# Layer 0's latents in two halves: loads in another order, and the products over the lower 512 channels before chunks 1 and 3 of the modulation

## Chip, cores and metric

The kernel runs on one core of a Trainium2 chip. The metric is the device time of one execution in microseconds (us); what is compared are medians over runs.

## What is computed

Two layers of a hybrid backbone over 640 tokens of 1024 channels: 512 latent tokens (`x_sample`) and 128 context tokens (`x_prompt`). Only the head of layer 0 matters here:

```python
m_lat = jnp.split((jax.nn.silu(c) @ mod_w[l] + mod_b[l])[:, None, :], 6, axis=-1)
m_ctx = jnp.split(jax.nn.silu(c_ctx) @ mod_w[l] + mod_b[l], 6, axis=-1)
hs = xs * (1.0 + m_lat[1]) + m_lat[0]          # and hp from xp with m_ctx
q_a, f_f, f_b, i_a, g_a, cq, ckv_raw, kr = jnp.split(h @ w_in, AB_SPLITS, axis=-1)
q = (_rms_norm(cq_raw, q_norm_g) @ w_uq)       # 384 columns of cq
ckv = _rms_norm(ckv_raw, kv_norm_g)            # 256 columns, then 32 of kr
```

Shift and scale (`m[0]`, `m[1]`) are the first 2048 columns of `mod_w[0]`, four chunks of 512: chunks 0 and 1 are the shift of channels 0 to 511 and 512 to 1023, chunks 2 and 3 the scale of the same halves. The "latents" are the last 672 columns of `h @ w_in` (384 + 256 + 32). All is float32. What follows (attention, HGRN2, experts, layer 1) is not touched.

## The kernel before

The program for each engine is written out by hand; engines meet at semaphores. PSUM is cut into four slots of 128x1024 words. `psum_groups()` lists every group of matmuls in PE's order and hands the slots out in turn (slot 0, 1, 2, 3, 0, ...); `open_group` makes PE wait until the group that had the slot before has been released by the engine that reads it, `filled` makes a reader wait for PE, `release` and `emptied` are the other way round.

**Loads.** SP issues all large loads in the order of a list `items`, each into one of five weight slots of 2 MB; `load_item` first waits (`retire`) until PE has closed the last group that read the slot's old content. Before: the first 131 columns of the constants, `mod` chunks 0 to 3 (2 MB each, slots 0 to 3), token tiles 0 and 1 of X, the lower half of `cqa` (512 latent columns, channels 0 to 511, 1 MB), its upper half, `cqb` (the other 160 columns, 0.64 MB), token tiles 2 and 3, tile 4, the other constants (1.2 MB), `uq`, `ukv`. ACT's own queue issues eleven small loads for the vectors, the first two of which are `c` and `c_ctx`; POOL's issues six.

**PE.** It waits for all small vectors and the Silu on ACT (L1055), turns the vectors into columns (group `vec`, L2319 to L2321), and then, by `FIRST_MODS`, multiplies the columns of silu(c) by the weight chunks (`mod`, L2174, eight matmuls over 512 columns) and turns each result row, once DVE has copied it out (L1441), into columns (`modb`, L2183, four matmuls of two columns). The order is `mod` 0, `mod` 1, `modb` 0, `mod` 2, `modb` 1, `mod` 3, `modb` 2, X tile 0, `modb` 3, so that a turn has another product ahead of it.

**A token tile.** PE turns the eight 128x128 blocks of X (`xT`, L2196). ACT evacuates blocks 0 to 3 with scale and shift (L1022), DVE blocks 4 to 7 (L1473). PE multiplies by `cqa` and `cqb` over eight blocks of channels (`cq`, L2350, L2354, L2358 for tile 0 and L2295 for the others). ACT copies the 672 columns out (L1075), squares and sums them (L1077, L1078) and takes the roots (L1079, L1080); DVE takes reciprocals and scales (L1522 to L1525). PE turns the normed rows (`nT`, L2211 to L2216) one tile later and computes the values (`v`, L2340) of the tile before that. `nT` 5 is the cached context, `krP` (L2379) the rotation of the rope keys.

In the trace a float32 matmul stands as two records, so a group of 16 matmuls reads x32; a transpose is one record. In the profile X is `x_tm`, the turned and modulated X is `h_cm`, slots 0 to 2 are `weights`, slot 3 is `mix_cm`, `c_cm` holds silu(c), `mod_parts` the result rows, and `scratch` the latents and what is made of them.

## Time and profile before

| | us |
|---|---|
| median of 3 runs | 1297.8 |
| lowest, highest | 1297.08, 1301.81 |
| the profiled execution, its own time | 1300.3 |
| its span | 1298.4 |
| PE busy | 1197.1 (92%) |
| DVE, ACT, POOL busy | 598.1, 352.1, 193.5 |
| mean granted clock of PE | 0.97 |

The profile is of one execution. Its rows give a start and a duration in us from the start of the span; what stands in brackets is how long the engine was idle ahead and what released it. The part that the change touches is the first 100 us of 1298.

### The profile page before, as it was taken

Reading aid. Unit: us, or ns where it says so; the run is one execution under the profiler, and the core shown is the slowest. Engines: PE = TensorE matmul, PEld = TensorE weight load, DVE = VectorE, ACT = ScalarE, POOL = GpSimd, SP = SyncE. Lnnn points to the kernel's source line nnn. Section 1 sums busy time; section 2 is a strip of 40 time slices with the busy share of each in tenths; the row PEclk is TensorE's granted clock in tenths of the full one; section 3 lists DMA queues with packets and bytes.
Section 4 is the critical chain, followed back from the end, with each engine's and each line's share of the span. In section 5 each row is a group of like instructions: output and inputs, shape, how many; then the busy total and the mean of one; then the engine's idle time right before and its main releaser. Section 6 shows DMA issues by size and latency. Waiting matters only on the chain.

```text
span 1298.4 us, 17510 instructions
## 1 busy us (share of the span) xinstructions
PE 1197.1 (92%) x6755; PEld 682.6 (53%) x6755; DVE 598.1 (46%) x1173; ACT 352.1 (27%) x695; POOL 193.5 (15%) x189
## 2 busy tenths in 40 slices
PE   5999999999999989999999868999999999999774
PEld 2554555545546677455555435755555555555431
DVE  2213333310136666857332217079986866322218
ACT  1333444421214543212122115311023111121122
POOL 1000000010000001231332120800000333232220
PEclk9999999999999999998999898999999998999977
DMA  9504467873110205816799959021114338999873
GB/s 350 204 28 173 151 242 253 283 256 136 66 62 10 74 9 208 325 70 254 309 409 408 407 206 359 23 90 65 66 65 183 141 147 309 407 410 407 347 265 138
DMA packets 99666, 269.79 MB, mean 208 GB/s; under 512 B 12811, under 2 KB 15154, under 8 KB 98690
## 3 DMA queue, kind: packets, MB, share of 16 engines
q1 hardware_dynamic: 81904, 228.26, 46.7%
q0 software_dynamic: 17360, 40.31, 8.5%
q8 instruction: 54, 0.88, 0.3%
q14 instruction: 26, 0.21, 0.0%
q10 hardware_dynamic: 322, 0.12, 0.0%
HBM read 257.68 MB, written 31.93 MB: 223 GB/s over the span
## 4 chain that ended last, share of the span: by engine, by line
PE 76%; DMA 7%; DVE 6%; SPq 5%; ACT 3%; issue 2%; ACTq 0%; POOL 0%; POOLq 0%; DVEq 0%
PE ps L2284 17%; PE ps L2295 14%; PE ps L2796 8%; PE ps L2174 4%; PE ps L2813 3%; DMA ln_rows<-in_moe_w_up 3%; PE ps L2436 3%; PE ps L2599 3%; PE ps L2784 2%; SPq L710 2%; PE ps L2580 2%; SPq L708 2%; PE ps L2403 2%; PE ps L2226 1%; DMA scratch<-expert_rows 1%
## 5 line engine op out<-in xcount | busy, mean ns | idle before, releaser
L2284 PE MATMUL ps<-h_cm,weights 128*128 128x512 f32 (+1 forms) x832 | 226.8, 434 | 0.0
L2284 PEld LDWEIGHTS ps<-h_cm,weights 128*128 128x128 f32 x832 | 126.3, 191 | 104.0 <-issue 103.7
L2295 PE MATMUL ps<-weights,mix_cm 128*128 128x512 f32 x256 | 112.2, 595 | 0.0
L1768 DVE SCALAR_TENSOR_TENSOR scratch<-scratch,taps_cm 128x655 f32<-128x655 f32 x120 | 101.5, 897 | 2.5 <-ACT scratch L1324 1.0
L2295 PEld LDWEIGHTS ps<-weights,mix_cm 128*128 128x128 f32 x256 | 47.9, 190 | 56.5 <-issue 56.4
L2066 DVE TENSOR_TENSOR scratch<-ps,scratch 128x128 f32<-128x128 f32 x38 | 11.1, 291 | 142.3 <-ACT scratch L1372 142.3
L2295 PE MATMUL ps<-weights,h_cm 128*128 128x512 f32 (+1 forms) x208 | 71.4, 502 | 0.0
L2796 PE MATMUL ps<-weights,scratch 128*64 128x256 f32 x384 | 70.1, 395 | 0.2 <-DMA weights<-in_moe_w_up 0.2
L1441 DVE COPY mod_parts<-ps 128x512 f32<-128x512 f32 x24 | 16.6, 690 | 94.0 <-PE ps L2174 94.0
L1696 DVE SCALAR_TENSOR_TENSOR mix_cm<-mix_cm,gate_rows,ps 128x128 f32<-128x128 f32 x152 | 46.0, 345 | 25.1 <-PE ps L2544 23.0
L921 POOL DMA_INDIRECT expert_rows<-scratch,gather_scatter_rows x32 | 31.9, 998 | 158.3 <-ACT scratch L1362 98.9
L2295 PEld LDWEIGHTS ps<-weights,h_cm 128*128 128x128 f32 x208 | 36.3, 190 | 35.6 <-issue 35.6
L2796 PE MATMUL ps<-h_cm,scratch 128*64 128x256 f32 x208 | 49.2, 391 | 6.3 <-DMA ln_rows<-in_moe_w_up 4.7
L2796 PE MATMUL ps<-scratch 128*64 128x256 f32 x192 | 48.0, 407 | 5.9 <-DMA weights<-in_moe_w_up 5.9
L2058 DVE COPY scratch<-ps 128x512 f32<-128x512 f32 x38 | 26.3, 691 | 51.2 <-PE ps L2813 46.4
L1372 ACT ACTIVATE scratch<-ps 128x128 f32<-128x128 f32 x38 | 10.5, 277 | 143.4 <-PE ps L2796 143.4
L902 POOL DMA_DIRECT2D h_rows<-scratch x10 | 5.6, 558 | 279.4 <-DVE scratch L1854 279.4
L2796 PEld LDWEIGHTS ps<-weights,scratch 128*64 128x64 f32 x384 | 40.4, 142 | 7.1 <-DMA weights<-in_moe_w_up 0.4
L1573 DVE TENSOR_REDUCE softmax_max<-ps 128x1 f32<-128x640 f32 (+1 forms) x40 | 26.8, 711 | 30.3 <-PE ps L2436 30.1
L1354 ACT ACTIVATE scratch<-ps 128x512 f32<-128x512 f32 x38 | 22.7, 597 | 63.2 <-PE ps L2784 62.6
L2796 PEld LDWEIGHTS ps<-h_cm,scratch 128*64 128x64 f32 x208 | 28.2, 140 | 21.6 <-issue 8.9
L1362 ACT ACTIVATE scratch<-ps 128x512 f32<-128x512 f32 x38 | 22.7, 597 | 59.9 <-PE ps L2813 54.5
(451 smaller groups left out, 2149.0 us busy)
## 6 DMA issues: line engine op xcount, KB each, us to landing
weights<-in_mod_w SPq DMA_DIRECT2D x13, 2048.0 KB, 8.4
x_tm<-in_mod_w SPq DMA_DIRECT2D x10, 2048.0 KB, 8.6
weights<-in_moe_w_gate SPq DMA_DIRECT2D x24, 512.0 KB, 11.1
weights<-in_moe_w_up SPq DMA_DIRECT2D x24, 512.0 KB, 13.5
weights<-in_moe_w_down SPq DMA_DIRECT2D x24, 512.0 KB, 15.3
scratch<-in_moe_w_down SPq DMA_DIRECT2D x21, 512.0 KB, 13.3
weights<-in_ab_w_in SPq DMA_DIRECT2D x5, 2048.0 KB, 12.9
weights<-in_cd_w_in SPq DMA_DIRECT2D x5, 2048.0 KB, 18.5
```

What stands on the lines that cost most here:

```text
L921: nc.gpsimd.indirect_dma_start(out=YD[:, :], out_offset=bass.IndirectOffsetOnAxis(ap=rows, axis=0), in_=ZT[:, par, :], in_offset=None, bou ...
L1573: V.tensor_reduce(MXS[:, b, i:i + 1], ps("s", h, t)[:, 0:nk], AX.X, ALU.max, negate=True).then_inc(softmax_dve, 1)
L1696: ins = V.scalar_tensor_tensor(out=nxt, in0=state_before(i, n, step, hh), scalar=HE[:, u % 2, at:at + 1], in1=bank(4 + j)[:, hh * 128:hh * ...
L1768: ins = V.scalar_tensor_tensor(out=CO[:, j, 0:655], in0=UP[:, j, k:k + 655], scalar=CW[:, 4 * k + j:4 * k + j + 1], in1=CO[:, j, 0:655], o ...
L2058: V.tensor_copy(ZT[:, u % 2, 512:1024], result_bank(u, 1)).then_inc(m["yv"], 1)
L2174: ins = T.matmul(ps("mod", l, c)[32 * j:32 * j + 32, 0:512], CT[:, k, :], w[:, k, :], start=(k < 4), stop=(k >= 4))
L2284: ins = T.matmul(ps(*name)[:, a:b], w[:, k, col:col + 128], HT[:, k, a:b], start=(k == 0), stop=(k == KD - 1))
L2295: ins = T.matmul(ps(*name)[:, at:at + w.shape[2]], src[:, k, t * 128:t * 128 + 128], w[:, k, :], start=(k == 0), stop=(k == KD - 1))
L2436: ins = T.matmul(ps("s", 2 * p + i, t)[:, a:b], q[rows, tc], k[rows, ka:ka + b - a], start=(rope == 0), stop=(rope == 1))
L2599: ins = T.matmul(bank(3)[:, 0:256], HT[:, k, t * 128:t * 128 + 128], w[:, k, 256 * half:256 * half + 256], start=(k == 0), stop=(k == KD - 1))
L2796: ins = T.matmul(pair_bank(u)[SL * i:SL * i + SL, 0:256].rearrange("p (g f) -> p g f", g=2), XGT[:, u % 2, at:at + SL], w[:, k, :, :], sta ...
L2813: ins = T.matmul(result_bank(u, b)[SL * i:SL * i + SL, :], HIDT[:, u % 2, SL * i:SL * i + SL], w[:, b * 512:b * 512 + 512], start=True, st ...
```

## The change

It does five things.

1. SP's order becomes: constants, chunk 0 (slot 0), chunk 2 (slot 2), X tiles 0 and 1, the lower half of `cqa` (slot 1, free so far), then, once PE has done the product with chunk 2, the lower half of `cqb` (slot 2), X tiles 2 and 3, chunk 1 (slot 3), chunk 3 (slot 0), the upper halves of `cqa` and `cqb`, X tile 4, constants, `uq`, `ukv`.
2. `c` and `c_ctx` get a semaphore of their own (`d_c`). The Silu waits for these alone, and PE turns them in a group of their own (`c`) ahead of the other vectors.
3. The latents of a tile are made in two halves. `xa` t (blocks 0 to 3 of X) is evacuated by ACT, `ca` t multiplies it by the lower halves of the weights into a PSUM slot and ACT copies the 672 columns out. Later `xT` t (blocks 4 to 7) is evacuated by DVE, `cq` t multiplies by the upper halves, and DVE adds the first half while it copies out.
4. PE's order up to `ca` 4 is the list `FRONT`.
5. Semaphores: `xT` groups are released by DVE, so `h_half` is gone from the loop; `d_cache` is merged into `d_vec`.

```diff
-FIRST_MODS = [("mod", 0), ("mod", 1), ("modb", 0), ("mod", 2), ("modb", 1), ("mod", 3), ("modb", 2), ("modb", 3)]
+FRONT = [("c",), ("mod", 0, 0), ("vec",), ("modb", 0, 0), ("mod", 0, 2), ("modb", 0, 2), ("xa", 0), ("xa", 1), ("ca", 0), ("xa", 2), ("ca", 1),
+         ("xa", 3), ("ca", 2), ("mod", 0, 1), ("modb", 0, 1), ("ca", 3), ("mod", 0, 3), ("modb", 0, 3), ("xa", 4), ("xT", 0, 0), ("ca", 4)]
...
-        for c in range(4):
-            mod_item(0, c, c)
+        for c, at in ((0, 0), (2, 2), (1, 3), (3, 0)):
+            mod_item(0, c, at)
...
-                    if items[n] == ("cqa",):
-                        retire(WITEM[items[n]]["before"])
+                    if items[n] == ("mod", 0, 1):
+                        sp.dma_start(X[:, 0:2, :], xs[:, 0:2, :]).then_inc(d_x[0], 16)
+                        sp.wait_ge(d_first, 16)
                         sp.dma_start(cqa_to[:, 0:4, :], cqa_from[:, 0:4, :]).then_inc(d_first, 16)
+                        retire(("mod", 0, 2))
+                        sp.dma_start(cqb_to[:, 0:4, :], cqb_from[:, 0:4, :]).then_inc(d_first, 16)
+                        sp.dma_start(X[:, 2:4, :], xs[:, 2:4, :]).then_inc(d_x[1], 16)
                     load_item(n)
...
+            def first_half(t):
+
+                filled(act, "ca", t)
+                release(A_(CQ[:, t, :], ps("ca", t)[:, 0:672], ACT.Copy), "ca", t)
...
-            act.wait_ge(d_vec_a, 16 * 11)
+            act.wait_ge(d_c, 32)
...
             h_evac0(0)
-            h_evac0(1)
             for t in range(NT):
-                filled(act, "cq", t)
-                release(A_(CQ[:, t, :], ps("cq", t)[:, 0:672], ACT.Copy), "cq", t)
+                if t + 1 < NT:
+                    h_evac0(t + 1)
+                first_half(t)
+            for t in range(NT):
                 emptied(act, "cq", t)
...
-            for kind, c in FIRST_MODS:
-                drain_mod(kind, 0, c)
+            for c in (1, 3):
+                mod_row(0, c)
+                mod_columns(0, c)
...
             for t in range(NT):
+                if t + 1 < NT:
+                    h_evac0(t + 1)
+                filled(dve, "cq", t)
+                release(V.tensor_tensor(CQ[:, t, :], ps("cq", t)[:, 0:672], CQ[:, t, :], ALU.add), "cq", t)
                 if t:
                     turned_queries(t - 1)
...
+            def latents(name, t, ks):
+
+                open_group(pe, *name)
+                for at, w in ((0, wa), (512, wb)):
+                    for k in ks:
+                        ins = T.matmul(ps(*name)[:, at:at + w.shape[2]], HT[:, k, t * 128:t * 128 + 128], w[:, k, :],
+                                       start=(k == ks[0]), stop=(k == ks[-1]))
+                close_group(ins, *name)
+
+            for name in FRONT[3:]:
+                if name[0] in ("mod", "modb"):
+                    side(*name)
+                elif name[0] in ("xa", "xT"):
+                    x_turn0(name, name[-1])
+                else:
+                    emptied(pe, "xa", name[1])
+                    pe.wait_ge(d_first, 48)
+                    latents(name, name[1], range(0, 4))
+            weights(pe, "cqa")
+            weights(pe, "cqb")
             for t in range(NT):
-                if t:
-                    emptied(pe, "xT", 0, t)
-                    pe.wait_ge(h_half, t + 1)
-                    project_tm(("cq", t), HT, t, [(0, wa), (512, wb)])
-                if t + 2 < NT:
-                    x_turn0(t + 2)
+                if t + 1 < NT:
+                    x_turn0(("xT", 0, t + 1), t + 1)
+                emptied(pe, "xT", 0, t)
+                latents(("cq", t), t, range(4, KD))
                 turn_normed(t - 1 if t else NT)
```

**PE, the start of the kernel.** L2319 to L2321 are the vectors, L2174 a `mod` product, L2183 a `modb` turn, L2196 X's transposes, L2350 and L2354 the latents of tile 0. Before:

```order
L2319 MATMUL ps<-consts,gate_rows 128x96
L2320 MATMUL ps<-consts,gate_rows 128x44
L2321 MATMUL ps<-consts,gate_rows 128x124
L2174 MATMUL ps<-weights,c_cm 32x512 x16
L2183 MATMUL ps<-consts,mod_parts 128x2 x4
L2174 MATMUL ps<-weights,c_cm 32x512 x8
L2183 MATMUL ps<-consts,mod_parts 128x2 x4
L2174 MATMUL ps<-mix_cm,c_cm 32x512 x8
L2183 MATMUL ps<-consts,mod_parts 128x2 x4
L2196 MATMUL ps<-consts,x_tm 128x128 x8
L2183 MATMUL ps<-consts,mod_parts 128x2 x4
L2350 MATMUL ps<-weights,h_cm 128x512 x4
```

The same place in the changed kernel (L2323 is the group `c`, L2181 a product, L2330 to L2332 the vectors, L2190 a turn, L2203 X's transposes, L2355 the latents):

```order
L2323 MATMUL ps<-consts,gate_rows 128x16
L2181 MATMUL ps<-weights,c_cm 32x512 x8
L2330 MATMUL ps<-consts,gate_rows 128x96
L2331 MATMUL ps<-consts,gate_rows 128x44
L2332 MATMUL ps<-consts,gate_rows 128x124
L2190 MATMUL ps<-consts,mod_parts 128x2 x4
L2181 MATMUL ps<-weights,c_cm 32x512 x8
L2190 MATMUL ps<-consts,mod_parts 128x2 x4
L2203 MATMUL ps<-consts,x_tm 128x128 x8
L2355 MATMUL ps<-weights,h_cm 128x512 x4
```

One product stands ahead of the vectors, two of the four products are gone from the place, and each turn stands right behind its product.

**PE, from `ca` 3 to `ca` 4 in the changed kernel**, with what each waits for; nothing like it was there before. L2355 is `ca` 3 and, below, `ca` 4; L2181 the product with chunk 3, L2190 its turn; the first L2203 is `xa` 4, the second `xT` 0.

```order
L2355 MATMUL ps<-weights,h_cm 128x160 x4
L2181 MATMUL ps<-weights,c_cm 32x512 [waits slot_free0,w_full0]
L2181 MATMUL ps<-weights,c_cm 32x512 x7
L2190 MATMUL ps<-consts,mod_parts 128x2 [waits slot_free1,slot_free0]
L2190 MATMUL ps<-consts,mod_parts 128x2 x3
L2203 MATMUL ps<-consts,x_tm 128x128 [waits slot_free2,d_x0]
L2203 MATMUL ps<-consts,x_tm 128x128 x3
L2203 MATMUL ps<-consts,x_tm 128x128 [waits slot_free3,d_x0]
L2203 MATMUL ps<-consts,x_tm 128x128 x3
L2355 MATMUL ps<-weights,h_cm 128x512 [waits slot_free0,d_first,slot_free2]
```

`xT` 0 waits for PSUM slot 3, which `ca` 3 has.

**ACT in the changed kernel, from `xa` 3 on**, with the slots it waits for. L1020 is the evacuation of an `xa`, L1027 the copy of a `ca`.

```order
L1020 ACTIVATE h_cm<-ps,mod_cols 128x128 [waits slot_full3]
L1020 ACTIVATE h_cm<-ps,mod_cols 128x128 x3
L1027 ACTIVATE scratch<-ps 128x672 [waits slot_full0]
L1020 ACTIVATE h_cm<-ps,mod_cols 128x128 [waits slot_full2]
L1020 ACTIVATE h_cm<-ps,mod_cols 128x128 x3
L1027 ACTIVATE scratch<-ps 128x672 [waits slot_full3]
L1027 ACTIVATE scratch<-ps 128x672 [waits slot_full0]
```

The copy of `ca` 3 (slot 3) stands behind the evacuation of `xa` 4 (slot 2).

## Rows read from the trace of the kernel before

**Rows 1.** The page: busy us (share of the span) xinstructions, and the chain by engine.

```profile
PE 1197.1 (92%) x6755; PEld 682.6 (53%) x6755; DVE 598.1 (46%) x1173; ACT 352.1 (27%) x695; POOL 193.5 (15%) x189
...
PE 76%; DMA 7%; DVE 6%; SPq 5%; ACT 3%; issue 2%; ACTq 0%; POOL 0%; POOLq 0%; DVEq 0%
```

**Rows 2.** The chain in order of time: start us, us, what.

```profile
5.32 8.60 DMA gate_rows<-in_ln_b
...
42.36 0.87 PE ps L2196 x8
...
81.55 0.33 PE ps L2211 x3
...
82.46 1.91 PE ps L2340 x4
84.37 9.04 PE ps L2295 x32
```

**Rows 3.** PE's timeline: start us, us, operation, count, [idle before <-releaser].

```profile
17.72 6.53 PE L2174 MATMUL ps<-weights,c_cm 128*32 128x512 f32 x32 [1.31 <-DVE taps_cm L1493]
24.18 1.05 PE L2183 MATMUL ps<-consts,mod_parts 128*128 128x2 f32 x8
...
28.00 1.92 PE L2174 MATMUL ps<-mix_cm,c_cm 128*32 128x512 f32 x16
...
30.77 1.07 PE L2196 MATMUL ps<-consts,x_tm 128*128 128x128 f32 x8
...
33.56 5.37 PE L2350 MATMUL ps<-weights,h_cm 128*128 128x512 f32 x8 [0.93 <-ACT h_cm L1022]
```

**Rows 4.** Loads issued at 1.18, 6.54, 12.77, 24.32: count, KB, us to landing.

```profile
weights<-in_mod_w SPq DMA_DIRECT2D x1, 2048.0 KB, 9.5
mix_cm<-in_mod_w SPq DMA_DIRECT2D x1, 2048.0 KB, 20.7
x_tm<-in_x_sample SPq DMA_DIRECT2D x1, 1024.0 KB, 17.1
weights<-in_ab_w_in SPq DMA_DIRECT2D x1, 1024.0 KB, 8.2
```

**Rows 5.** Products (ns min/median/max), then stretches: us, PE busy (records), granted clock, DMA share, GB/s.

```profile
L2174 PE MATMUL ps<-weights,c_cm x8: 1057/1060/1061, 17.7 to 18.6; 128*32 128x512 f32 x8
L2174 PE MATMUL ps<-weights,c_cm x12: 593/968/1061, 22.0 to 23.7; 128*32 128x512 f32 x12
...
34.00:35.00 1.00, 1.00 (x2) 0.50 1.11 319
37.00:37.50 0.50, 0.50 (x3) 0.76 1.02 401
...
602.80:603.70 0.90, 0.90 (x8) 1.00 0.98 319
603.90:605.30 1.40, 1.40 (x8) 0.50 1.07 415
```

**Rows 6.** Timelines of ACT and DVE: start us, us, line, operation, [idle before].

```profile
24.33 0.69 DVE L1441 COPY mod_parts<-ps 128x512 f32<-128x512 f32 x1 [2.14 <-PE ps L2174]
45.45 0.73 ACT L1075 ACTIVATE scratch<-ps 128x672 f32<-128x672 f32 x1 [0.67 <-PE ps L2358]
47.24 1.28 ACT L1079 ACT_TABLE_LOAD   x1
48.54 0.30 ACT L1079 ACTIVATE rms_scale<-square_sums,rms_eps 128x1 f32<-128x1 f32 x1
49.86 0.48 DVE L1525 SCALAR_TENSOR_TENSOR scratch<-scratch,rms_scale 128x256 f32<-128x256 f32 x1
97.50 0.69 DVE L1534 TENSOR_TENSOR scratch<-ps,consts 128x512 f32<-128x512 f32 x1 [0.52 <-PE ps L2379]
```

**Rows 7.** Behind the last `cq`: the turned rows on ACT, `krP` on PE.

```profile
95.91 0.26 ACT L1033 ACTIVATE scratch<-ps 128x128 f32<-128x128 f32 x1
96.27 1.10 PE L2379 MATMUL ps<-scratch,consts 128*128 128x512 f32 x2
```

More of the change, by code:

```diff
@@ L160, in psum_groups @@
 def psum_groups():
-    g = [("vec",)]
+    g = list(FRONT)
     for l in range(2):
         if l == 0:
-            g += [(kind, 0, c) for kind, c in FIRST_MODS[:-1]]
-        if l == 0:
-            g.append(("xT", 0, 0))
-            g += [(kind, 0, c) for kind, c in FIRST_MODS[-1:]]
             for t in range(NT):
+                if t + 1 < NT:
+                    g.append(("xT", 0, t + 1))
                 g.append(("cq", t))
-                if t == 0:
-                    g.append(("xT", 0, 1))
-                if t + 2 < NT:
-                    g.append(("xT", 0, t + 2))
                 g.append(("nT", t - 1 if t else NT))
@@ L1463, in mod_columns @@
                                                op0=ALU.add, op1=ALU.add), "modb", l, c)
-            def drain_mod(kind, l, c):
-                {"mod": mod_row, "modb": mod_columns}[kind](l, c)
             def h_evac0(t):
@@ L1484, in _ @@
             steps[0] += 1
+            filled(dve, "c")
+            dve.wait_ge(vec_step, steps[0])
+            release(V.tensor_copy(CT[:, :, 0:2], ps("c")[:, 0:16].rearrange("p (g k) -> p k g", g=2)), "c")
+            mod_row(0, 0)
             filled(dve, "vec")
-            dve.wait_ge(vec_step, steps[0])
-            chain(V.tensor_copy(CT[:, :, 0:2], ps("vec")[:, 192:208].rearrange("p (g k) -> p k g", g=2)))
             chain(V.tensor_copy(MBC[:, :], ps("vec")[:, 208:240]))
@@ L2188, in side, with x_turn0 @@
                 {"mod": mod_product, "modb": mod_turn}[kind](l, c)
-            def x_turn0(t):
-                pe.wait_ge(d_x[0 if t < 2 else 1], 16 if t < 2 else 32)
-                at_least(pe, h_half, t if t > 1 else 0)
-                open_group(pe, "xT", 0, t)
-                for k in range(KD):
-                    ins = T.transpose(ps("xT", 0, t)[:, k * 128:k * 128 + 128], X[:, t, k * 128:k * 128 + 128], ident)
-                close_group(ins, "xT", 0, t)
+            def x_turn0(name, t):
+                pe.wait_ge(d_x[1 if t in (2, 3) else 0], 32 if t == 4 else 16)
+                open_group(pe, *name)
+                first = 0 if name[0] == "xa" else 4
+                for k in range(4):
+                    ins = T.transpose(ps(*name)[:, k * 128:k * 128 + 128], X[:, t, (first + k) * 128:(first + k) * 128 + 128], ident)
+                close_group(ins, *name)
             def turn_normed(t):
@@ L2314, in _ @@
             pe.wait_ge(d_first, 16)
+            pe.wait_ge(c_silu, 1)
+            open_group(pe, "c")
+            close_group(T.matmul(ps("c")[:, 0:16], V1[0:16, :], C[0:16, 0:16], start=True, stop=True), "c")
+            emptied(pe, "c")
+            side("mod", 0, 0)
             pe.wait_ge(d_vec, 16 * 6)
-            pe.wait_ge(d_vec_a, 16 * 11)
-            pe.wait_ge(c_silu, 1)
+            pe.wait_ge(d_vec_a, 16 * 9)
+            open_group(pe, "vec")
             v = ps("vec")
@@ L2321, in _ @@
             close_group(T.matmul(v[:, 64:188], V3[:, :], C[0:124, 0:124], start=True, stop=True), "vec")
-            emptied(pe, "vec")
-            for kind, c in FIRST_MODS[:-1]:
-                side(kind, 0, c)
-            x_turn0(0)
-            side(FIRST_MODS[-1][0], 0, FIRST_MODS[-1][1])
             wa, wb = w8(slot3(WITEM[("cqa",)]["slot"])), w8(slot3(WITEM[("cqb",)]["slot"]), AB_IN - 3072)
```

78 lines of the change are left out of this document (31 added, 47 removed).

## Prediction

> **What bounds the kernel now.** I read four views, in this order. The page's busy shares and its chain by engine come first: PE is busy 92% of the span and makes up 76% of the chain that ended last [rows 1]. The chain in order of time shows what the first 94 us hang on: until 14.40 the small vector loads (the last `ln_b` lands at 13.92) and the Silu behind them, and from then on PE itself, but for one evacuation by ACT before 33.56 [rows 2, 3]. The timeline of PE gives each piece of that stretch: it idles 1.31 us before the first product with the modulation weights (17.72) and 0.93 us before the first latents (33.56), and not otherwise up to the end of the last `cq` product, 84.37 + 9.04 = 93.41 [rows 2, 3]. The issues and their times to landing say whether the loads press: the fourth 2 MB weight chunk lands at 6.54 + 20.7 = 27.2 and its product starts at 28.00, the first rows of X land at 12.77 + 17.1 = 29.9 and are turned at 30.77, the lower half of `cqa` lands at 24.32 + 8.2 = 32.5 and is used at 33.56 [rows 3, 4]. So from 17.7 on PE is full, and the loads run 1 us ahead of it. What the change can gain is therefore small: PE's idle time before 33.56 and the 3.3 us of one product that can be done before 14 us. It can't gain the 22 us for which the lower half of the latents runs beside loads, since that work only takes the place of other PE work.
>
> **When things land afterwards.** The first chunk lands where it does now, 1.18 + 9.5 = 10.7, and from 10.7 to 27.2 three more came: 5.5 us for 2 MB [rows 4]. By that rate chunk 2 lands at 16.2, X's first rows at 19, the lower half of `cqa` at 22. SP then waits for the product with chunk 2 (about 21, below) before it issues the lower half of `cqb`; 1 MB is still in flight then, and I put it at 23.5 to 24. Chunk 1 then lands near 33, chunk 3 near 38, the upper halves near 42. PE asks for them at about 43, 51 and 59. So behind `ca` 0 no load is waited for.
>
> **The change, part by part**, as PE's time from 14.4 to the end of the last `cq`, which is 79.0 us now (to 93.41). Everything later in the first 100 us hangs on that end, and SP frees the slot of the next weight chunk by it, so a shift there goes through to the end at par.
>
> Saved:
> - The product with chunk 0 needs only `c`, which now has its own semaphore. No row shows when `c` lands. It is the first load on ACT's queue; even with the 8.6 us of the queue's last [rows 2] it and a short Silu are done when chunk 0 lands, at 10.7, and there the product starts. It takes 6.53/2 = 3.27 us [rows 3] and ends at 14.0. Saved: 3.27 us, and 0.3 us because the vector products no longer follow the Silu.
> - The idle 1.31 us behind the vector products is filled by the turn of chunk 0: saved 1.3. The idle 0.93 before the first latents goes too (its successor is counted below). In all 5.8 us.
>
> Added:
> - The clock. The first two products run at 1057 ns a matmul, the later ones at 593 [rows 5]: 6.53 us for two against 1.92 for one. By these durations the first two are at the low one of the clock's two levels. Now chunks 0 and 1 pay this (1.35 us each), afterwards chunks 0 and 2: no difference. But the turns of chunks 0 and 2 and the turning of X tile 0 fall into it too. Eight small matmuls (one row of eight at each level) took 0.90 us at the high level and 1.40 at 0.50 [rows 5], so a turn, 0.98 to 1.05 at the high level [rows 3], costs 0.45 more and the four transposes 0.25: **1.15 us** (0, if the clock is up by then, to 1.6).
> - Turns without cover. A turn needs the row that DVE copies: 0.69 us, 0.1 behind the product's end (24.33 against 24.25) [rows 3, 6], 0.9 with the way back. Now another product runs meanwhile; afterwards the turns of chunks 2, 1 and 3 stand directly behind their products. 3 x 0.9 = **2.7 us**.
> - `ca` 0 waits for ACT's four evacuations of `xa` 0. Now these take from the transposes' end, 31.84, to 33.56, 1.72 us. The turning of tile 1 covers 0.5 to 0.9 of it: **1.0 us**. `ca` 0 so starts near 25.4, not at 33.56.
> - The clock under the latents. The low level held from 33.56 to about 37.1 under the first latents, 3.56 us or a loss of 1.8; at the start of the kernel it held from 17.72 until the records turn short at about 23.4, 5.7 us or a loss of 2.9 [rows 3, 5]. `ca` 0 lies behind small work and waits, so I take 2.3 against the 1.8 of now: **0.5 us** (-1.8 to 1.1).
> - The place before `ca` 4. ACT's program is the evacuation of `xa` 4, then the copy of `ca` 3, then the copy of `ca` 4. `ca` 3 holds the PSUM slot that `xT` 0 needs (slot 3, as the list of groups hands them out in turn). So PE turns `xa` 4, waits for the evacuation (1.72 with its latencies) and for the copy of 128x672 (0.73 [rows 6]), turns `xT` 0 in 0.44 and only then starts `ca` 4. **2.5 us** idle.
> - The clock there. From the end of chunk 3's product PE does nothing dense for 0.9 + 0.98 + 0.44 + 2.5 + 0.44 = 5.3 us. Now, between 29.92 and 33.56, it did nothing dense for 3.6 us, and the granted clock was 0.50 right after [rows 3, 5]. So I expect it to fall again: **1.8 us** by the spell of now (0 to 2.9).
> - DVE's add in place of a copy by ACT. 128x512 from PSUM took 0.69 [rows 6], so 672 columns some 0.86 to 0.9, 0.15 more than the copy. Within the loop it hides: a tile now has 0.44 + 4.52 + 0.91 + 1.91 = 7.8 us of PE work (halves of 0.87 and 9.04, the turn from 81.55 to 82.46, the values) [rows 2], and the chain from the start of the copy to the normed rows takes 49.86 + 0.48 - 45.45 = 4.9 us with a table load in it [rows 6], 5.1 with the add. The tightest is tile 0: PE asks for it 0.58 (the context's turn, 0.91 without its first 0.33) + 0.44 + 4.52 = 5.5 us after the end of `cq` 0. At the last tile the turned rows come out at 96.17 now and PE goes on at 96.27 [rows 7], so there is no slack: **0.2 us**.
>
> Number and kind of the latents' own matmuls stay: 16 to a tile, in two halves. Sum: -5.8 + 1.15 + 2.7 + 1.0 + 0.5 + 2.5 + 1.8 + 0.2 = **+4.0 us**. The profiled execution took 1300.3 (span 1298.4) and so would take 1304.3; it stands 2.5 us above the median of the runs, 1297.8, and against that I forecast **1301.8 us**. A measurement of this kernel can tell a change of about 0.5%, 6.5 us, from none, so this counts as the same.
>
> **A rule weighed.** The load of the Sqrt table in tile 0's chain took 1.28 us and the activation behind it started 1.30 us after it began [rows 6]; nothing more shows, and the sum goes by that.
> The Trainium skill, "ScalarE: Activation LUTs", section "What ACT_TABLE_LOAD costs", speaks against it: about 2.66 us for a switch, load and a drain of 1.38. By that the chain would be 6.5 us and the sum +5.0.
>
> **Rivals.**
> - *No second fall of the clock.* All as above, but the stretch before `ca` 4 doesn't count as idle: +2.2, 1300.0 us. For it: transposes stand in it, and where it lies in time is chance. Against it: a shorter stretch sufficed before.
> - *The clock is up early.* The product at 10.7 may bring the high level forward to the product with chunk 2. That saves 1.35 there, 1.15 on the small ones and 2.3 under `ca` 0, and with no fall before `ca` 4 another 1.8: -2.6, 1295.2 us. Against it: in the trace the level rose only after 5.7 us of unbroken products, and here vector products and waits lie between.
> - *Slower, by too many low spells.* One mechanism, PE's clock: besides the falls above it falls in the gap behind chunk 1's product too (0.9 + 0.98 = 1.9 us; 1.8), and the spells under `ca` 0 and `ca` 4 last like that at the kernel's start (0.6 and 1.1): +7.5, 1305.3. It decides from 2.5 us above my sum, that is from a third spell on. Against it: no stretch as short as 1.9 us was followed by a fall so far.
> - *The chain of tile 0 is late.* If the switch of tables costs 1.4 us more than its row shows, PE waits 1.0 us at the first turning of normed rows: 1302.8. Against it: the row.
> - *The loads bind after all.* SP holds back `cqb` and everything behind it until chunk 2's product is done. If the engines ran dry and `cqb` took the 8.2 us of the `cqa` row from its issue at 21, `ca` 0 would start at 29.3: 3.9 us later than above, 1305.7 us. Against it: behind it the row had 3 MB in flight ahead, here 1 MB.
> - *It does what its order suggests*: half of the latents hidden beside loads, 93.41 earlier by over 6.5 us. Against it: PE has 0.93 us of idle time there, not 20.
>
> **How the numbers follow.** Forecast 0.42, no second fall 0.22, early clock 0.12, many low spells 0.10, late chain 0.04, loads 0.06, the full gain 0.03; 0.01 for the rest. Runs of now spread from 1297.1 to 1301.8. The range, from the early clock's time to just past the third spell: 1295.0 to 1306.5. Faster by over 0.5% (below 1291.3): 0.03. Slower by over 0.5% (above 1304.3): the many spells (0.10) and most of the loads' case (0.04), 0.14. Same: 0.83.
>
> **What would show it.** In the new profile: the first product at about 10.7; `ca` 0 at 25 to 26 with a granted clock of 0.50 in its first microseconds; gaps of 0.9 us behind the three products; a wait for ACT before `xT` 0 and 0.50 under `ca` 4; from there 7.8 us a tile with no idle time; the last `cq` ended near 97.5. The forecast is wrong where the last `cq` ends before 92 or after 100, or where PE waits for a load behind 26 us.

## The result, and the profile after

| | before | after |
|---|---|---|
| median of 20 runs each | 1298.34 us | 1303.91 us |
| lowest, highest | 1296.8, 1302.19 | 1297.76, 1306.55 |
| profiled execution, its own time | 1300.3 | 1300.42 |
| its span | 1298.4 | 1298.5 |

The ratio is 1.0038 (95%: 1.0026 to 1.0051), 4.9 us slower. That is within 0.5% and counts as the same, as forecast, and its sign and size are those of the sum (+4.0). The two profiled executions differ by 0.1 us only; where the difference went is read below.

The page of after, busy shares and chain by engine; they answer to [rows 1] and look the same:

```profile
PE 1198.0 (92%) x6757; PEld 684.0 (53%) x6757; DVE 602.5 (46%) x1178; ACT 352.0 (27%) x695; POOL 193.5 (15%) x189
...
PE 75%; DMA 8%; DVE 7%; SPq 5%; ACT 3%; issue 3%; POOL 0%; POOLq 0%; DVEq 0%; ACTq 0%
```

The timeline of PE, after, which answers to [rows 3]: start us, us, operation, count, [idle before <-releaser]. L2181 is a `mod` product, L2190 a turn, L2203 X's transposes, L2330 one of the vector products, L2355 the latents of either half.

```profile
10.55 3.64 PE L2181 MATMUL ps<-weights,c_cm 128*32 128x512 f32 x16 [2.49 <-DMA weights<-in_mod_w]
14.12 0.74 PE L2330 MATMUL ps<-consts,gate_rows 96*128 96x96 f32 x2
...
15.95 1.71 PE L2190 MATMUL ps<-consts,mod_parts 128*128 128x2 f32 x8
17.59 3.64 PE L2181 MATMUL ps<-weights,c_cm 128*32 128x512 f32 x16
22.05 1.87 PE L2190 MATMUL ps<-consts,mod_parts 128*128 128x2 f32 x8 [0.82 <-DVE mod_parts L1443]
23.78 1.95 PE L2203 MATMUL ps<-consts,x_tm 128*128 128x128 f32 x8
26.55 6.52 PE L2355 MATMUL ps<-weights,h_cm 128*128 128x512 f32 x16 [0.82 <-ACT h_cm L1020]
...
38.30 4.68 PE L2355 MATMUL ps<-weights,h_cm 128*128 128x512 f32 x16
...
45.72 1.05 PE L2190 MATMUL ps<-consts,mod_parts 128*128 128x2 f32 x8 [0.88 <-DVE mod_parts L1443]
...
54.07 1.05 PE L2190 MATMUL ps<-consts,mod_parts 128*128 128x2 f32 x8 [0.81 <-DVE mod_parts L1443]
54.99 0.64 PE L2203 MATMUL ps<-consts,x_tm 128*128 128x128 f32 x4
57.93 1.09 PE L2203 MATMUL ps<-consts,x_tm 128*128 128x128 f32 x4 [2.31 <-ACT scratch L1027]
58.81 5.67 PE L2355 MATMUL ps<-weights,h_cm 128*128 128x512 f32 x16
```

Every place that the prediction named is there. The first product starts as soon as chunk 0 is in, at 10.55. The turns of chunks 2, 1 and 3 have 0.81 to 0.88 us of idle time ahead of them. `ca` 0 waits 0.82 for ACT and runs 6.52 us where a half at the high level takes 4.7 (38.30). The column of the granted clock prints 1.00 there, not the 0.50 that was forecast; why the durations are read instead stands in the last section. PE idles 2.31 before `xT` 0, until ACT's copy of `ca` 3 releases the PSUM slot.

The windows of PE across that last wait, after: stretch, us, PE busy (records), granted clock, DMA share, GB/s.

```profile
56.00:57.00 1.00, 0.00 (x0) 1.00 1.00 393
57.00:57.50 0.50, 0.00 (x0) 0.88 1.03 412
57.50:58.00 0.50, 0.07 (x1) 0.50 1.08 428
60.50:61.00 0.50, 0.50 (x2) 0.71 0.07 25
```

The granted clock falls at about 57.4, with PE idle, and comes back within 60.5 to 61. It is the second fall that the prediction put there. Behind `ca` 4 a tile takes 7.8 us (its `cq` starts at 70.44, 78.21, 85.99) and PE doesn't idle, as forecast.

The chain of waits, after: start us, us, what. It answers to the last row of [rows 2].

```profile
93.49 4.52 PE ps L2355 x16
```

The last `cq` ends at 98.01, 4.6 us later than before (93.41), and the lag of each later piece stays +4.7 up to 240 us. It is +2.9 at 567 and +0.5 at 1032. The profiled execution of before ran at the low level from 467.3 to 470.7, where that of after did not, and in two spells near 730 and 780 for 13.6 us together where after did for 6.8. That is 10.2 us more at the low level, against 4.2 us by which the lag shrinks. PE's timeline and windows at the first of these, before, in the same columns:

```profile
466.20 0.71 PE L2526 MATMUL ps<-x_tm 128*128 128x128 f32 x4 [2.08 <-DVE gate_rows L1686]
...
467.00:468.00 1.00, 1.00 (x6) 0.66 0.07 16
468.00:470.00 2.00, 2.00 (x6) 0.50 0.00 0
```

PE is full while the level is low, but the fall at 467.3 stands 1.1 us behind a wait of 2.08 us for DVE. At the same place after waits 1.73 us (before 470.76), and its level doesn't fall. The change doesn't touch this part. Such spells account for the two profiled executions being equal: at 1032 us, behind them, after is only 0.5 us late. The medians over 20 runs depend less on one execution's luck and show the 4.9; the profiled execution of after is one of its faster ones, 3.5 us below its median.

### The profile page after: what moved, and what is told of

The parts are those of the page before. It is cut to its first block, busy times and chain, and to the rows that moved or that the text cites. A ratio compares the mean times of both kernels' runs of the same rounds, so it can differ in the third digit from the quotient of the medians.

```text
span 1298.5 us, 17529 instructions
## 1 busy us (share of the span) xinstructions
PE 1198.0 (92%) x6757; PEld 684.0 (53%) x6757; DVE 602.5 (46%) x1178; ACT 352.0 (27%) x695; POOL 193.5 (15%) x189
## 4 chain that ended last, share of the span: by engine, by line
PE 75%; DMA 8%; DVE 7%; SPq 5%; ACT 3%; issue 3%; POOL 0%; POOLq 0%; DVEq 0%; ACTq 0%
PE ps L2290 17%; PE ps L2301 11%; PE ps L2802 7%; PE ps L2355 4%; PE ps L2181 4%; PE ps L2819 3%; PE ps L2442 3%; DMA ln_rows<-in_moe_w_up 3%; PE ps L2605 2%; PE ps L2790 2%; DMA weights<-in_mod_w 2%; SPq L702 2%; DMA scratch<-in_moe_w_up 2%; PE ps L2586 2%; PE ps L2409 2%
## 5 line engine op out<-in xcount | busy, mean ns | idle before, releaser
L2355 PE MATMUL ps<-weights,h_cm 128*128 128x512 f32 (+1 forms) x160 | 49.8, 465 | 0.8 <-ACT h_cm L1020 0.8
L1374 ACT ACTIVATE scratch<-ps 128x128 f32<-128x128 f32 x38 | 10.5, 277 | 143.9 <-PE ps L2802 143.9
L2355 PEld LDWEIGHTS ps<-weights,h_cm 128*128 128x128 f32 x160 | 27.6, 198 | 22.5 <-issue 21.3
## 6 DMA issues: line engine op xcount, KB each, us to landing
weights<-in_moe_w_up SPq DMA_DIRECT2D x24, 512.0 KB, 13.6
```

What stands on the lines that cost most here:

```text
L2355: ins = T.matmul(ps(*name)[:, at:at + w.shape[2]], HT[:, k, t * 128:t * 128 + 128], w[:, k, :], start=(k == ks[0]), stop=(k == ks[-1]))
```

## The experiments

**The theory**: the saving at the start is real (some 6 us), and three added costs outweigh it: turns without cover, the copy of `ca` 3 behind the evacuation of `xa` 4, and PE's clock, which falls where PE idles. **The rivals**: the loads in their new order bind; the clock at the start of the kernel decides alone; or the early product is worth nothing.

All are compared by ratio with the kernel before, run alongside on the same chip (medians of 1298.2 to 1299.0 us over 29 to 35 runs). "End" is the end of the last `cq` in the profile, 93.41 before and 98.01 after. Where PE multiplies data that nobody uses, the output doesn't depend on it.

| run | ratio (95%) | us against before | forecast | median us | end | forecast |
|---|---|---|---|---|---|---|
| copy_first | 1.0011 (0.9995 to 1.0027) | +1.4 | +3.3 | 1300.56 | 96.61 | 96.4 |
| dense_gap | 1.0014 (0.9999 to 1.0029) | +1.8 | none given | 1301.66 | 94.05 | 97.0 |
| covered_turns | 1.0023 (1.0012 to 1.0035) | +3.0 | +3.3 | 1301.66 | 92.35 | 96.4 |
| early_c | 1.0027 (1.0012 to 1.0042) | +3.5 | -0.9 | 1301.78 | 94.10 | 92.5 |
| late_c | 1.0054 (1.0030 to 1.0077) | +7.0 | +9 | 1306.08 | 103.94 | 102.4 |
| covered_all | 0.9998 (0.9982 to 1.0014) | -0.3 | -1 to -3 | 1298.04 | 90.42 | 92.2, or 88 with the clock up |
| warm_start | 1.0021 (1.0006 to 1.0035) | +2.7 | 0 | 1300.10 | 97.24 | 93 to 95 |
| covered_warm | 0.9983 (0.9967 to 0.9999) | -2.2 | -5 | 1296.00 | 90.17 | 87.5 to 89 |
| slots_all | 0.9985 (0.9969 to 1.0001) | -1.9 | -2 | 1296.86 | 90.04 | 89 to 93 |
| slots_warm | 0.9983 (0.9969 to 0.9996) | -2.2 | -4.5 to -5 | 1295.32 | 88.04 | 88.2 |
| before_warm | 1.0002 (0.9990 to 1.0015) | +0.3 | -1 or none | 1299.20 | 91.22 | 92.5 |

The changed kernel itself was not run again beside them, so its 4.9 us come from the 20 runs above. The forecasts of `early_c` and `warm_start` were missed in both columns. The gain of `covered_warm` and `slots_warm` over before came out at less than half of what was forecast, and `covered_all` gained nothing over before.

### The wait before `ca` 4: copy_first and dense_gap

`copy_first` has ACT copy `ca` 3 before it evacuates `xa` 4, so the PSUM slot comes free while PE still turns.

```diff
                 if t + 1 < NT:
+                    if t == 3:
+                        first_half(t)
                     h_evac0(t + 1)
-                first_half(t)
+                if t != 3:
+                    first_half(t)
```

> The changed kernel with one swap in ACT's program: the copy of `ca` 3 stands ahead of the evacuation of `xa` 4. My theory (the wait of 2.31 us before `xT` 0 at 57.93 is the PSUM slot of `ca` 3, held by ACT's order): `ca` 3 is copied at about 51.5 to 52.2, `xT` 0 follows `xa` 4 at once (55.6), only the evacuation of `xa` 4 (55.66 to 57.16) is waited for, `ca` 4 starts at 57.2 in place of 58.8, the last `cq` ends at 96.4 in place of 98.0; against the kernel before +3.3 us in place of +4.9. Rival (PE waits there for the evacuation alone, or for X tile 4): `ca` 4 starts at 58.8 as before and the last `cq` ends at 98.0.

PE's timeline, `copy_first` (L2206 are the transposes, L2358 the latents):

```profile
26.52 7.63 PE L2358 MATMUL ps<-weights,h_cm 128*128 128x512 f32 x16 [0.82 <-ACT h_cm L1020]
...
56.06 1.07 PE L2206 MATMUL ps<-consts,x_tm 128*128 128x128 f32 x8
58.30 4.79 PE L2358 MATMUL ps<-weights,h_cm 128*128 128x512 f32 x16 [1.16 <-ACT h_cm L1020]
```

Both groups of transposes now stand together (x8), the wait before `ca` 4 is 1.16 in place of 2.31 and `ca` 4 takes 4.79 in place of 5.67: no fall of the clock. `ca` 0 was 1.11 us longer here than in after, which has nothing to do with the edit; without that the end would be 95.5. So the order of two instructions on ACT was worth 2.5 us at this place. By the ratios the time is 3.5 us under that of after (+1.4 for +4.9), with intervals that just meet.

`dense_gap` leaves the wait and only lets PE multiply in it, two matmuls into the slot of `ca` 4, whose result `ca` 4 overwrites:

```diff
             for name in FRONT[3:]:
...
                 elif name[0] in ("xa", "xT"):
+                    if name == ("xT", 0, 0):
+                        open_group(pe, "ca", 4)
+                        for i in range(2):
+                            T.matmul(ps("ca", 4)[:, 0:512], ident, wa[:, 0, :], start=True, stop=True)
```

> The changed kernel with two matmuls of 512 columns without use put between `xa` 4 and `xT` 0, into the PSUM slot that `ca` 4 takes later; they fit into the wait of 2.3 us. My theory (the granted clock falls at 57.4 because PE has done nothing dense since 53.3): no fall there, `ca` 4 takes 4.7 us in place of 5.67, its start stays at 58.8, the last `cq` ends at 97.0 in place of 98.0. Rival (the fall has another cause, or so short a piece of dense work does not change it): granted clock 0.50 near 57.4 all the same, `ca` 4 5.7 us, 98.0. If the two matmuls themselves run at the low level they last 3.4 us and everything is about 1 us later.

PE's timeline, `dense_gap`, in the same columns:

```profile
52.90 1.88 PE L2366 MATMUL ps<-weights,consts 128*128 128x512 f32 x4
55.37 0.63 PE L2203 MATMUL ps<-consts,x_tm 128*128 128x128 f32 x4 [0.59 <-ACT scratch L1027]
55.84 4.69 PE L2355 MATMUL ps<-weights,h_cm 128*128 128x512 f32 x16
```

The wait for ACT lasts as long as before (1.88 + 0.59 against 2.31), but the transposes behind it take 0.63 in place of 1.09 and `ca` 4 4.69 in place of 5.67. The loss of 1.4 us is thus the clock's, and it comes from PE's idleness, not from ACT. (The transposes start 2.6 us sooner than in after because this execution had the high level at the second product, see below; `ca` 0 started 3.8 us sooner and then gave 1.3 back, 7.78 us for 6.52.)

The other profiles bear this out. Of the ten changed versions, four idle 2.31 us before `xT` 0, and in all four the level fell: `ca` 4 took 5.67 us in after, 5.82 in `covered_turns`, 5.64 in `late_c` and 6.38 in `warm_start`. In the six in which the wait is filled or at most 1.16 us long it took 4.69 to 4.79. The place of the fall varies: in `warm_start` it comes at about 57.5, 0.7 us after the wait is over.

### The turns without cover: covered_turns and covered_all

`covered_turns` puts `xa` 0 ahead of `modb` 2 and `ca` 2 ahead of `modb` 1. `covered_all` also covers `modb` 3 and puts more between `xa` 4 and `ca` 4:

```diff
-FRONT = [..., ("modb", 0, 2), ("xa", 0), ("xa", 1), ("ca", 0), ("xa", 2), ("ca", 1), ("xa", 3), ("ca", 2), ("mod", 0, 1), ("modb", 0, 1), ("ca", 3), ("mod", 0, 3), ("modb", 0, 3), ("xa", 4), ("xT", 0, 0), ("ca", 4)]
+FRONT = [..., ("xa", 0), ("modb", 0, 2), ("xa", 1), ("ca", 0), ("xa", 2), ("ca", 1), ("xa", 3), ("mod", 0, 1), ("ca", 2), ("modb", 0, 1), ("mod", 0, 3), ("ca", 3), ("xa", 4), ("modb", 0, 3), ("xT", 0, 0), ("ca", 4)]
```

> The changed kernel with PE's list in another order at two places: the turning of X tile 0 stands between the product with chunk 2 and its turn, and the product with chunk 1 is moved ahead of `ca` 2, its turn behind `ca` 2. The place before `ca` 4 is left as it is. My theory (a turn that stands right behind its product costs PE a gap of 0.8 to 0.9 us each, and nothing else was won by it): no gap of 0.82 at 21.3 and none of 0.88 at 44.9, `ca` 0 starts at 25.9 in place of 26.55, the last `cq` ends at 96.4 in place of 98.0; against the kernel before +3.3 us. Rival (the loads take the gap's place: chunk 1 lands at 36.5 and is now asked for at about 37): PE waits for chunk 1 and the last `cq` ends at 97 or later.

> The changed kernel with PE's list in another order, so that no turn and no evacuation is without other work: chunk 2's product, `xa` 0, its turn, `xa` 1, `ca` 0; chunk 1's product, `ca` 2, its turn, chunk 3's product, `ca` 3, `xa` 4, its turn, `xT` 0, `ca` 4. Nothing else is changed. My theory (the change's loss is gaps in PE's program, 0.82 + 0.88 + 0.81 behind products and 2.31 before `xT` 0, and one fall of the clock, 1.0): all of it goes, the last `cq` ends at about 92.2 where the first products run at the low level and near 88 where they don't, against the kernel before -1 to -3 us. Rival (other waits, for chunk 1, chunk 3 or X tile 4, take the gaps' place): the last `cq` ends at 95 or later.

PE's timeline, `covered_turns` (L2180 a product, L2202 transposes, L2354 latents):

```profile
16.35 1.92 PE L2180 MATMUL ps<-weights,c_cm 128*32 128x512 f32 x16 [0.23 <-DMA weights<-in_mod_w]
...
22.66 4.76 PE L2354 MATMUL ps<-weights,h_cm 128*128 128x512 f32 x16 [1.80 <-ACT h_cm L1019]
...
52.12 1.08 PE L2202 MATMUL ps<-consts,x_tm 128*128 128x128 f32 x4 [2.31 <-ACT scratch L1026]
53.00 5.82 PE L2354 MATMUL ps<-weights,h_cm 128*128 128x512 f32 x16
```

In its profiled execution the second product took 1.92 us, not 3.64, and `ca` 0 4.76, not 6.52. That is the rival with the clock up early, and it is no effect of the edit: the products with chunks 0 and 2 are issued as in after. The early level makes much of the end of 92.35. Over 13 runs the time is 3.0 us above before (1.0023) where after's is 4.9 (1.0038): 1.9 us for two covered turns, where 2 x 0.9 of the prediction's terms give 1.8; the intervals overlap.

PE's timeline, `covered_all`:

```profile
23.58 6.48 PE L2354 MATMUL ps<-weights,h_cm 128*128 128x512 f32 x16 [1.35 <-ACT h_cm L1019]
...
52.13 4.76 PE L2354 MATMUL ps<-weights,h_cm 128*128 128x512 f32 x16 [1.02 <-ACT scratch L1026]
```

All three turns are covered, the wait before `ca` 4 is 1.02 in place of 2.31, and there is no second fall. The end is 90.42, 7.6 us sooner than in after. Of this, 3.0 us stand ahead of `ca` 0 (23.58 for 26.55): the covered turn gives 0.8, a wait for ACT that is 0.5 longer takes part of it back, and the other 2.7 are the clock in this execution. The two turns took 0.96 and 1.05 us for 1.71 and 1.87 in after, and the second product 3.33 for 3.64, though `ca` 0 itself was as slow as in after (6.48). The 4.6 us behind the start of `ca` 0 are the edit's: 0.88 + 0.81 of turns, 1.3 of wait and 1.4 of clock make 4.4. So the edit is worth 4.9 us in the profile and 5.2 in the ratios (-0.3 for +4.9, intervals apart). The time is that of before (0.9998): with those terms of the sum taken out the slowdown is gone.

### Part 2 alone, and part 2 taken back: early_c and late_c

`early_c` is before with the early Silu, the group `c` and `mod` 0 ahead of the other vectors, and no other load order. (The change merges two semaphores since the program has none left, and so does this.)

```diff
-    g = [("vec",)]
+    g = [("c",), ("mod", 0, 0), ("vec",)]
...
-            act.wait_ge(d_vec_a, 16 * 11)
+            act.wait_ge(d_c, 32)
```

> The kernel before with part 2 of the change alone: `c` on its own semaphore, turned ahead of the other vectors, and the product with chunk 0 ahead of them; order of loads and latents as before. Theory A (PE is full from 17.7 on, but the loads run only 1 us ahead of it): the product starts at 10.6, later products wait for chunks 1 to 3 (landing at 16.6, 21.8, 27.2), X's first rows at 29.9 and the lower half of `cqa` at 32.5; the first latents start at 32.6 in place of 33.56, the last `cq` ends at 92.5 in place of 93.4, -0.9 us against the kernel before. Theory B (PE alone bounds the place): the saved 5 us come through, the latents start at 29 and the last `cq` ends at 88.5, -5 us.

PE's timeline, `early_c` (L2178 are the four products):

```profile
10.53 3.38 PE L2178 MATMUL ps<-weights,c_cm 128*32 128x512 f32 x16 [2.60 <-DMA weights<-in_mod_w]
...
16.58 3.36 PE L2178 MATMUL ps<-weights,c_cm 128*32 128x512 f32 x16 [1.30 <-DMA weights<-in_mod_w]
...
27.41 3.47 PE L2178 MATMUL ps<-mix_cm,c_cm 128*32 128x512 f32 x16 [2.50 <-DMA mix_cm<-in_mod_w]
```

PE is ahead of the loads now and waits for each chunk, 2.50 us for the fourth; the clock falls there as well, and that product takes 3.47 us for 1.92. The end is 94.10, not sooner than before. In before's load order the early product gains nothing, since the fourth chunk at 27.2 and X behind it bind [rows 4]. Only with the new order is the 3.3 us a saving. By the ratio the time is 3.5 us above before, more than the 0.7 at the end; why is not settled. One candidate is what the semaphores forced: POOL's loads of the cached context now wait for its first six loads and share their semaphore. Every changed version has that too, and no run has it alone.

`late_c` is after with a Silu that waits for all vectors again:

```diff
             act.wait_ge(d_c, 32)
+            act.wait_ge(d_vec_a, 16 * 9)
```

> The changed kernel, but the Silu waits for all of ACT's small loads, as before. The sum counted 5.8 us saved at the start. My theory: the product with chunk 0 starts at 15 in place of 10.55, the one with chunk 2 at about 22 in place of 17.6, everything behind it is 4.4 us later, the last `cq` ends at 102.4, +9 us against the kernel before. Rival (the loads set the start of `ca` 0 anyhow): `ca` 0 starts within 2 us of 26.55 and the last `cq` ends at 98 to 100.

ACT's timeline, `late_c`: start us, us, operation, [idle before].

```profile
13.99 1.28 ACT L1059 ACT_TABLE_LOAD   x1 [13.99 <-DMA gate_rows<-in_ln_b]
```

PE's timeline, `late_c`:

```profile
16.58 3.64 PE L2182 MATMUL ps<-weights,c_cm 128*32 128x512 f32 x16 [0.27 <-DVE c_cm L1487]
...
32.59 6.45 PE L2356 MATMUL ps<-weights,h_cm 128*128 128x512 f32 x16 [0.82 <-ACT h_cm L1020]
```

The first product starts 6.0 us later than in after (16.58 for 10.55), `ca` 0 6.0 later (32.59 for 26.55), and the end is 5.9 later. Up to the last `cq` a delay at the start goes through at par. The table load went behind the wait too and makes 1.3 of the 6. The time is 7.0 us above before by the ratio, with 3 us to either side, so 2.1 more than after where the end says 5.9 more, and the two intervals overlap. The early Silu is worth 6 us up to the last `cq` in the profile; what it is worth in the median is not shown.

### The clock at the start: warm_start, before_warm

`warm_start` is after with multiplications of zeros ahead of chunk 0's arrival and around its product (`Z` is a zeroed tile):

```diff
+            def idle_work(count, n, *name):
+                open_group(pe, *name)
+                for i in range(count):
+                    T.matmul(ps(*name)[:, 512:512 + n], Z[:, 0:128], Z[:, 0:n], start=True, stop=True)
+            idle_work(4, 512, "c")
...
+            idle_work(2, 256, "mod", 0, 0)
...
+            idle_work(2, 256, "vec")
```

> The changed kernel with matmuls without use in PE's idle time: four of 512 columns from about 1.5 us on, two of 256 ahead of the product with chunk 0 and two behind it. My theory (in the profile of the changed kernel the first two products, the two turns, X's first transposes and part of `ca` 0 run at the low level, together 6 to 7 us more than at the high one): the product with chunk 0 takes 1.9 us, the one with chunk 2 1.9, `ca` 0 starts at 22.7 and takes 4.7 to 7; the last `cq` ends at 93 to 95 in place of 98.0; the runs scatter less than those of the changed kernel; against the kernel before 0 us in place of +4.9. Rival (the low level at the start is not from idling): products of 3.6 us, last `cq` at 98.

PE's timeline, `warm_start` (L2326 the useless work, L2183 the products, L2367 the latents):

```profile
1.45 6.11 PE L2326 MATMUL ps<-scratch 128*128 128x512 f32 x8 [1.45 <-DVE scratch L1482]
10.58 1.92 PE L2183 MATMUL ps<-weights,c_cm 128*32 128x512 f32 x16 [1.30 <-DMA weights<-in_mod_w]
...
16.72 3.52 PE L2183 MATMUL ps<-weights,c_cm 128*32 128x512 f32 x16 [0.67 <-DMA weights<-in_mod_w]
...
24.29 7.72 PE L2367 MATMUL ps<-weights,h_cm 128*128 128x512 f32 x16 [1.24 <-ACT h_cm L1020]
...
57.33 6.38 PE L2367 MATMUL ps<-weights,h_cm 128*128 128x512 f32 x16
```

The first product is at the high level (1.92), but the second is back at the low one: between them lie 4.2 us with two short useless matmuls, the vectors, a turn and two waits. `ca` 0 starts 2.3 us sooner than in after and takes 7.72 us for 6.52, which leaves 1.1 us; the end is 97.24 (98.01).

`before_warm` is before with 11 such matmuls ahead of the vectors:

```diff
+            for i in range(11):
+                T.matmul(ps("vec")[:, 512:1024], Z[:, 0:128], Z[:, 0:512], start=True, stop=True)
```

> The kernel before with eleven matmuls of 512 columns without use from 1.5 us on, in the time in which PE waits for the small vectors. Theory A (in the order of before the loads run only 1 us ahead): the products with chunks 0 and 1 take 1.9 us each, but those with chunks 2 and 3 and the first latents wait for their loads (21.8, 27.2, 32.5), the last `cq` ends at 92.5, -1 us or none. Theory B (the low level at the start is what the kernel before loses there): the whole 2.7 us come through and more under the first latents, the last `cq` ends at 90 or before.

The eleven matmuls kept the clock up for little of what follows: the products with chunks 0 and 1 took 5.87 us together (6.53 before), not the 3.8 that theory A expected. The first latents took 3.67 us (5.37 before), without a spell of the low level. The end so comes 2.2 us sooner in its profile (91.22), while the time over 12 runs is unchanged (1.0002): one profile's end is no measure of the median to better than some 2 us.

### Together: covered_warm, slots_all, slots_warm

`covered_warm` is `covered_all` with the useless matmuls of `warm_start`. The other two also let `cqb` go into a slot that is free, so that SP waits for no product before it:

```diff
-        for c, at in ((0, 0), (2, 2), (1, 3), (3, 0)):
+        for c, at in ((0, 0), (2, 3), (1, 0), (3, 3)):
...
-                        retire(("mod", 0, 2))
```

> Both together: the list without gaps and the matmuls without use at the start. My theory: the first products run at the high level, `ca` 0 starts at about 22.6, no gap above 0.5 us but for the loads of X tiles 0, 2 and chunk 1; the last `cq` ends at 87.5 to 89 in place of 93.4 (before) and 98.0 (changed); -5 us against the kernel before, and it beats both. Rival (what is won at the start is lost to the loads, which then come last): the last `cq` ends at 91 or later, -2 us.

> slots_warm without the matmuls without use at the start: what the order and the slots give by themselves. My theory: `ca` 0 starts at 23 to 26, by how long the low level holds at the start, and takes 4.7 to 7.7; the last `cq` ends at 89 to 93; against the kernel before -2 us. Rival (without work ahead the low level always holds up to 26 us): the last `cq` ends at 92.5 or later and the time is that of the kernel before.

> covered_warm with the weight slots handed out otherwise: chunk 2 and chunk 3 in slot 3, chunk 1 in slot 0, so that slot 2 is free and SP issues the lower half of `cqb` without waiting for chunk 2's product. My theory (in covered_warm the queue ran dry behind the wait at 19.8, `ca` 0 waited 1.5 us and chunk 1's product 1.4 us for loads): the loads run on without a hole, `ca` 0 starts at 22.9 in place of 23.57, no wait for chunk 1, the last `cq` ends at 88.2 in place of 90.2; against the kernel before -4.5 to -5 us. Rival (both waits are set by bandwidth, not by the hole): the last `cq` ends at 90.

The windows that gave the edit its reason, after: SP waits for chunk 2's product before it issues `cqb`, and the DMA engines run dry. Columns: stretch, us, busy time of the five engines PE, PEld, DVE, ACT, POOL, then clock, DMA share, GB/s.

```profile
20.00:21.00 1.00, 1.00 (x8) 0.00 (x0) 0.00 (x0) 0.00 (x0) 0.00 (x0) 1.00 0.22 82
21.00:22.00 1.00, 0.23 (x4) 0.00 (x0) 0.69 (x1) 0.00 (x0) 0.00 (x0) 1.00 0.03 12
22.00:23.00 1.00, 0.95 (x5) 0.95 (x5) 0.00 (x0) 0.00 (x0) 0.00 (x0) 1.00 0.50 59
```

In after PE waits for none of the loads behind this hole. PE's timeline, `covered_warm` (L2182 is the product with chunk 1):

```profile
35.14 1.92 PE L2182 MATMUL ps<-mix_cm,c_cm 128*32 128x512 f32 x16 [1.41 <-DMA mix_cm<-in_mod_w]
```

There PE is ahead of chunk 1 by 1.41 us. PE's timeline, `slots_warm`:

```profile
16.48 1.92 PE L2181 MATMUL ps<-mix_cm,c_cm 128*32 128x512 f32 x16 [0.63 <-DMA mix_cm<-in_mod_w]
...
22.92 4.76 PE L2365 MATMUL ps<-weights,h_cm 128*128 128x512 f32 x16 [1.91 <-ACT h_cm L1018]
...
33.01 1.92 PE L2181 MATMUL ps<-weights,c_cm 128*32 128x512 f32 x16
```

The product with chunk 1 starts at 33.01, without a wait. Here the second product and `ca` 0 both ran at the high level. `slots_warm` has the earliest end: its last `cq` ends 5.4 us sooner than before's (88.04), and its time is 2.2 us under before by the ratio (0.9983, 0.9969 to 0.9996), clear of before, if by little. `slots_all`, without the useless matmuls, is at 0.9985 (0.9969 to 1.0001), `covered_warm` at 0.9983: the three can't be told apart, so neither the free slot nor the useless matmuls at the start are shown to be worth anything in the median.

## Why the prediction held

The changed kernel came out at 1303.9 us where 1301.8 was forecast, in the range, and its ratio, 4.9 us, stands beside a sum of 4.0. By its steps, from the profile of after:

| step | forecast | measured | from |
|---|---|---|---|
| first product starts | 10.7 | 10.55 | timeline |
| its length | 3.3 | 3.64, almost all of it ahead of the vectors | timeline |
| small work at the low level | +1.15 | +2.0 | turns 1.71 and 1.87 against 0.98 and 1.05; half of 1.95 - 1.07 for `xa` 0 |
| three uncovered turns | +2.7 | +2.5 | 0.82 + 0.88 + 0.81 |
| `ca` 0 waits for ACT | +1.0 | +0.82 | timeline |
| `ca` 0 starts | 25.4 | 26.55 | timeline |
| low level under `ca` 0, loss | 2.3 | 1.8 | 6.52 - 4.68 |
| wait before `xT` 0 | +2.5 | +2.31 | timeline |
| second fall of the clock | +1.8 | +1.4 | 0.45 on the transposes, 5.67 for 4.7 on `ca` 4 |
| tail, with the add on DVE | +0.2 | +0.13 | `krP` 2.99 behind the last `cq`, 2.86 before |
| last `cq` ends | 97.5 | 98.01 | chain |

Every term stood at its place with its sign, but for the 0.5 that the low level under `ca` 0 was to cost more than before: it cost 1.8, as before. The term that was mis-sized most is the small work: I took 0.45 more for a turn, from eight small matmuls at either level [rows 5], and the two turns cost 0.7 and 0.8 more. The transposes of `xa` 0 cost 0.2 more, and the product with chunk 2 took 3.64 in place of 3.27. That makes the 1.1 us by which `ca` 0 started late; later terms were a little smaller than forecast and gave back half. That the sum came so near is partly luck, since `ca` 0 took from 4.76 to 7.78 us in the profiles of the changed versions, a loss of 0.1 to 3.1 us by the state of the clock.

One step is borne out in part only: that a shift of the last `cq` goes through to the end at par. For after it does (+4.6 at that end, +4.9 in the ratio), but over all twelve kernels a straight line through the shift of the end and the time by the ratio has a slope of 0.6: `late_c` +10.5 and +7.0, `slots_warm` -5.4 and -2.2. Each end is of one execution, with its own luck at the start, which flattens such a line; how much of the 0.6 is that stays open. Where the end is that of before, the line stands at +1.2 us (standard error 0.4). The sum has no term for such an offset; it may come from the merged semaphores or be chance, so the agreement of +4.6 and +4.9 may be luck in part.

The rivals. *No second fall* and *the clock is up early* each occur, but in other executions: the first when the wait is shorter or filled (`copy_first`, `dense_gap`), the second by chance (`covered_turns`, `dense_gap`). The level was high at the second product in two of the six versions whose PE program is the same up to there, more often than the 0.12 given to it. It didn't bring the 6.6 us that the rival counted: in `dense_gap` it fell again under `ca` 0 (7.78), in `covered_turns` before `ca` 4 (5.82). That it widens the spread of the runs is not shown: after's 20 runs spread over 8.8 us and before's 20 over 5.4, but before's 29 to 35 runs beside the experiments spread over 8.1 to 8.8. *Too many low spells*: two, not three; the 1.9 us behind chunk 1's product (45 to 46.6) brought none. *The chain of tile 0 is late* fell. ACT's timeline, after, answering to [rows 6]:

```profile
71.40 1.28 ACT L1083 ACT_TABLE_LOAD   x1
72.70 0.29 ACT L1083 ACTIVATE rms_scale<-square_sums,rms_eps 128x1 f32<-128x1 f32 x1
```

The activation starts 1.30 behind the table load's start, and the first turning of normed rows follows `cq` 1 without a wait. Had the switch cost the 2.66 us that the Trainium skill, "ScalarE: Activation LUTs", section "What ACT_TABLE_LOAD costs", states, PE would have waited 1.0; the measurement decides for the row. *The loads bind* fell for the change, but shows in `early_c` (2.50 us) and in `covered_warm` (1.41), where PE was made faster than the loads. *The full gain* fell: even the best version ends its last `cq` only 5.4 us sooner than before; the 20 us of latents beside the loads were never to be gained.

## What to carry to other kernels

Work that is started earlier "beside loads" gains only what the engine had idle there; here that was some 6 us, and the new order gave back more in three uncovered turns, one copy queued behind an evacuation, one fall of the clock and small work at the low level. When a loop is split in two halves, look in each engine's own order for the instruction that frees the buffer which the next group needs, and put it first: two lines on ACT were worth 2.5 us in the profile. In a wait of some 2 us that can't be removed, look whether the clock falls in it, and fill it with matmuls if it does.
